# A PEER decoder layer on one core: 42 instead of 32 dense tokens leave the dense down products, and VectorE forms five of the last lower halves

## The reference, cut to what matters

```python
SEQ, D_MODEL, PEER_HEADS, PEER_TOPK, PEER_N_EXPERTS = 512, 1024, 8, 16, 16384

# short convolution and HGRN2 heads -> output projection -> cross-attention into 256 memory tokens, then:
h = rmsnorm(x, ffn_norm_w)
x = x + peer_ffn(h, w_query, sub_keys, expert_down, expert_up)
return rmsnorm(x, final_norm_w)

def peer_ffn(...):
    # per token and head: top 16 of each half of the keys, then the top 16 of the 256 pairs, softmax gates
    u = jnp.take(expert_down, idx, axis=0)                 # 128 rows of 1024 for each token
    a = jax.nn.gelu(jnp.einsum('nd,nhkd->nhk', xb, u))
    w = gb * a
    v = jnp.take(expert_up, idx, axis=0)
    return jnp.einsum('nhk,nhkd->nd', w, v)
```

## Time and profile before

| | us |
|---|---|
| median of 3 runs (1622.50 to 1630.98) | 1624.84 |
| the profiled execution | 1624.01 |
| its span, first to last instruction | 1622.3 |
| TensorE busy | 1600.3 |
| VectorE busy | 1133.7 |
| GpSimd busy | 829.1 |
| ScalarE busy | 673.2 |

### The profile page before, as it was taken

One profiled execution on the slowest core, in us unless ns is written; L12 is line 12 of the kernel. 1 busy time (PEld: TensorE's weight loads), 2 busy tenths in 40 slices (PEclk: granted clock), 3 DMA queues, 4 the chain that ended last, 5 costly groups with the idle time before them and its releaser, 6 DMA issues.

```text
span 1622.3 us, 26556 instructions
## 1 busy us (share of the span) xinstructions
PE 1600.3 (99%) x9227; PEld 1422.6 (88%) x9227; DVE 1133.7 (70%) x2214; ACT 673.2 (41%) x998; POOL 829.1 (51%) x523
## 2 busy tenths in 40 slices
PE   8999999999999999999999999999999999999998
PEld 6888888788889999999999999998888888888886
DVE  4155451351509999996999898329888888888887
ACT  5342453451534343534545544444333333333333
POOL 4463276423244998987787777866422222222220
PEclk9999999999999999999999999999999999999999
DMA  4322242313434999997999999949999999999992
GB/s 184 93 100 71 75 151 94 104 53 117 146 102 131 347 340 332 329 335 233 339 405 394 387 403 401 362 158 391 400 348 350 331 349 339 349 334 348 339 331 77
DMA packets 154425, 424.69 MB, mean 262 GB/s; under 512 B 15728, under 2 KB 65904, under 8 KB 154224
## 3 DMA queue, kind: packets, MB, share of 16 engines
q1 hardware_dynamic: 89088, 229.41, 40.5%
q0 software_dynamic: 41472, 151.01, 25.5%
q10 hardware_dynamic: 23792, 43.33, 6.9%
HBM read 379.88 MB, written 43.25 MB: 261 GB/s over the span
## 4 chain that ended last, share of the span: by engine, by line
PE 69%; issue 16%; POOL 9%; DVE 2%; DMA 2%; ACT 1%; POOLq 0%; SPq 0%; ACTq 0%; DVEq 0%
PE psum L1471 22%; PE psum L1473 22%; PE psum L1472 22%; POOL w_low L461 8%; PE psum L1766 4%; DMA gate_dram<-arena 1%; DMA kept<-down_in 1%; POOL arena L493 1%; DMA arena<-down_rows,arena 0%; DVE arena L1258 0%; ACT w_high L581 0%; DVE arena L1202 0%; DVE arena L1193 0%; DVE arena L1194 0%; DMA kept<-front_w 0%
## 5 line engine op out<-in xcount | busy, mean ns | idle before, releaser
L461 POOL TENSOR_TENSOR w_low<-kept,w_high 128x1024 fp32r<-128x1024 f32 x212 | 519.5, 2454 | 320.3 <-ACT w_high L581 317.6
L1471 PE MATMUL psum<-hT_high,w_high 128*128 128x352 f32 (+2 forms) x1408 | 484.4, 344 | 7.2 <-POOL w_low L461 5.5
L1473 PE MATMUL psum<-hT_high,w_low 128*128 128x352 f32 (+2 forms) x1408 | 476.6, 339 | 0.0
L1472 PE MATMUL psum<-hT_low,w_high 128*128 128x352 f32 (+2 forms) x1408 | 476.4, 338 | 0.0
L581 ACT ACTIVATE w_high<-kept 128x1024 fp32r<-128x1024 f32 x212 | 224.0, 1058 | 202.6 <-DMA kept<-down_in 102.0
L1471 PE MATMUL psum<-up_high,wgt_high 128*128 128x512 f32 x768 | 298.8, 389 | 0.0
L1473 PE MATMUL psum<-up_high,wgt_low 128*128 128x512 f32 x768 | 298.8, 389 | 0.0
L1472 PE MATMUL psum<-up_low,wgt_high 128*128 128x512 f32 x768 | 298.8, 389 | 0.0
L1471 PEld LDWEIGHTS psum<-hT_high,w_high 128*128 128x128 f32 x1408 | 264.8, 188 | 24.2 <-POOL w_low L461 8.2
L1473 PEld LDWEIGHTS psum<-hT_high,w_low 128*128 128x128 f32 x1408 | 264.7, 188 | 12.7
L1472 PEld LDWEIGHTS psum<-hT_low,w_high 128*128 128x128 f32 x1408 | 264.8, 188 | 12.3 <-issue 0.5
(11 more groups left out here) (252 smaller groups left out, 1956.4 us busy)
## 6 DMA issues: line engine op xcount, KB each, us to landing
kept<-down_in SPq DMA_DIRECT2D x128, 512.0 KB
arena<-up_in SPq DMA_DIRECT2D x128, 512.0 KB, 4.7
kept<-front_w SPq DMA_DIRECT2D x92, 512.0 KB
gate_dram<-arena ACTq DMA_DIRECT2D x40, 512.0 KB
hid_dram<-arena ACTq DMA_DIRECT2D x112, 176.0 KB
arena<-hid_dram SPq DMA_DIRECT2D x112, 176.0 KB
under_w<-gate_dram SPq DMA_DIRECT2D x24, 640.0 KB
arena<-gate_dram SPq DMA_DIRECT2D x8, 640.0 KB
```

Source lines behind the costliest of these rows:

```text
L461: nc.gpsimd.tensor_tensor(w_low[:, s, :], ring[:, s, :], w_hi[:, s, :].bitcast(F32), ALU.subtract).then_inc(low_ready, 1)
L1471: nc.tensor.matmul(out, lhs[0], rhs[0], start=first, stop=False)
L1472: nc.tensor.matmul(out, lhs[0], rhs[1], start=False, stop=False)
L1473: return nc.tensor.matmul(out, lhs[1], rhs[0], start=False, stop=last)
```

## The change

EDGE goes from 32 to 42. The dense block is then 128 x 342, three groups of 42 tokens fill 126 partitions, and their 128 slots go into 43 gathers (43 + 43 + 42), which read 126 rows, the last one 84. ROWS goes from 160 to 171. The dots move between the stretches: 70 instead of 66 by the end of the early stretch (four more, DOTS_LULL, stand after the last choice, but their gathers are spread over the same blocks 2 to 53), 76 instead of 80 in the gate steps, 25 instead of 14 in the last blocks. VectorE makes the lower halves of blocks 109, 111, 113, 115 and 117 (`dve_low`) and TensorE waits for them by a semaphore of their own. GELU of the edge dots moves to step 16, the wait for its results to step 23. Each of the three small groups of DMAs has three transfers of 42 partitions for four of 32. TensorE's last 20 blocks are written out instead of a loop. Nothing else differs.

```diff
-EDGE = 32
+EDGE = 42
-EDGE_SLOTS = SLOTS // PARTS
+EDGE_SLOTS = -(-SLOTS // PARTS)
-E0, E_BASE = P - EDGE, P - 32
+E0, E_BASE = P - EDGE, P - 64
-GEL_AT, SPLIT_AT, LAST_TURN = 12, 20, 28
+GEL_AT, SPLIT_AT, LAST_TURN = 16, 23, 28
-DOTS_A = DT * (sum(DOTS_SCORES) + sum(DOTS_CAND) + DOTS_HOT)
-DOTS_STEP = (0, 0) + (2,) * 10 + (1, 2, 2) * 12
-DOTS_END = (1,) * 14
+DOTS_LULL = 4
+DOTS_A = DT * (sum(DOTS_SCORES) + sum(DOTS_CAND) + DOTS_HOT) + DOTS_LULL
+DOTS_STEP = (0, 0, 1) + (2, 2, 1) * 15
+DOTS_END = (2, 2) * 6 + (1,)
...
+        def dve_low(i):
+            return DURING <= i < DURING + 10 and i % 2 == 1
...
-                nc.gpsimd.indirect_dma_start(ring[slot], None, down_rows, bass.IndirectOffsetOnAxis(
-                    (edge_idx if edge else idx3)[:, j:j + 1].bitcast(U32), 0))\
+                rows = edge_rows(j) if edge else P
+                nc.gpsimd.indirect_dma_start(ring[slot][0:rows], None, down_rows, bass.IndirectOffsetOnAxis(
+                    (edge_idx if edge else idx3)[0:rows, j:j + 1].bitcast(U32), 0))\
...
-                low(FRONT + i, i % 4)
+                if not dve_low(i):
+                    low(FRONT + i, i % 4)
...
+            kd = dots(kd, DOTS_LULL)
             assert kd == DOTS_A
...
-            kd = dots(kd, ROWS - kd)
+            for i in range(DURING, DURING + len(DOTS_END)):
+                if dve_low(i):
+                    dve.wait_ge(high_ready, FRONT + i + 1)
+                    nc.vector.tensor_tensor(w_low[:, i % 4, :], ring[:, i % 4, :], w_hi[:, i % 4, :].bitcast(F32),
+                                            ALU.subtract).then_inc(end_low_ready, 1)
+                kd = dots(kd, DOTS_END[i - DURING])
...
-            with pe.Fori(DURING // 4, NK // 4) as r:
-                for s in range(4):
-                    first_product(r * 4 + s, s)
+            for i in range(DURING, NK):
+                if dve_low(i):
+                    pe.wait_ge(end_low_ready, sum(dve_low(j) for j in range(i + 1)))
+                first_product(i, i % 4, FRONT + sum(not dve_low(j) for j in range(i + 1)))
```

More of the change, by code:

```diff
@@ L214, in build @@
         hk_last, split_last = at(136.25, 2 * P, 2, P), at(26, 3 * P, 3, P)
-        edge_idx, edge_dot, edge_gel = (at(137.25 + 0.125 * j, EDGE_SLOTS) for j in range(3))
+        edge_idx, edge_dot, edge_gel = (at(137.25 + 0.25 * j, EDGE_SLOTS) for j in range(3))
         idx_last, edge_back = at(17, SLOTS), at(18, SLOTS)
@@ L253, in build @@
         high_ready = sem("high_ready")
-        low_ready = sem("low_ready")
+        low_ready, end_low_ready = sem("low_ready"), sem("end_low_ready")
         idx_ready = sem("idx_ready")
@@ L325, in __call__, with part_slots, part_count, edge_rows @@
                 self.end()
+        def dve_low(i):
+            return DURING <= i < DURING + 10 and i % 2 == 1
+        def part_slots(q):
+            return slice(q * EDGE_SLOTS, min((q + 1) * EDGE_SLOTS, SLOTS))
+        def part_count(q):
+            return min(EDGE_SLOTS, SLOTS - q * EDGE_SLOTS)
+        def edge_rows(j):
+            return EDGE * sum(j < part_count(q) for q in range(PARTS))
         block = ctx.enter_context(nc.Block())
@@ L1181, in dots @@
                         step(nc.vector.tensor_copy(h_chunks, own_h))
-                    nc.vector.tensor_tensor_reduce(ring[slot], ring[slot], h_row, 1.0, 0.0, ALU.mult, ALU.add,
-                                                   (edge_dot if edge else dot3)[:, j:j + 1]).then_inc(dot_done, 1)
+                    rows = edge_rows(j) if edge else P
+                    nc.vector.tensor_tensor_reduce(ring[slot][0:rows], ring[slot][0:rows], h_row[0:rows], 1.0, 0.0, ALU.mult, ALU.add,
+                                                   (edge_dot if edge else dot3)[0:rows, j:j + 1]).then_inc(dot_done, 1)
                 return first + count
@@ L1473, in three, with columns @@
                 return nc.tensor.matmul(out, lhs[1], rhs[0], start=False, stop=last)
-            def columns(b, s, rhs, n, bank):
-                pe.wait_ge(low_ready, b + 1)
+            def columns(b, s, rhs, n, bank, lows=None):
+                pe.wait_ge(low_ready, b + 1 if lows is None else lows)
                 for k in range(KC):
```

39 lines of the change are left out of this document (23 added, 16 removed).

## The result

The changed kernel takes 1663.8 us (median of 6 runs, 1648.0 to 1669.3) where the kernel before takes 1627.5 (6 runs): a ratio of 1.021, 95% interval 1.0187 to 1.0234. The forecast was 1627, its range ended at 1636. The prediction was wrong in size: it had the kernel 2.6 us slower and it is 36.3 us slower.

The account below looks back on a forecast made before the run. TensorE was taken as the bound, with GpSimd just behind in the early and last blocks. The terms +3.7 - 4.7 + 3.4 + 0.2 = +2.6 gave 1627 us on the median; forecast 1622 to 1631 (0.56), range 1614 to 1636.

Parts of the forecast that it names:

- Ten columns fewer: TensorE's first products: 0.42 ns a column, 0.10 us a block, 12.8 us less over 128 blocks.
- Early stretch, +3.7: Blocks 0 to 59: GpSimd's added gathers and dot waits outweigh the shorter products, 3.7 us longer.
- the dot waits of gathers 32 and 54: Early stretch: GpSimd waits for dots ahead of these moved gathers, about 2.9 us near 611 and 3.3 near 684.
- The prediction is wrong if the early stretch ends before 759: Test set for the early stretch: an end before 759 us would refute the prediction.
- Gate steps, -4.7: Blocks 60 to 107: TensorE's period falls from 5.29 to 5.19 us, less 0.1 for stores of gates: 4.7 us shorter.
- -4.8 to -3.5: Bounds in us given for the change of the gate steps, blocks 60 to 107.
- Last blocks, +3.4: Last 20 blocks: shorter products give -2.0, the ring of four row buffers and VectorE's halves +5.4: 3.4 us longer.
- The cycle of the ring: Last blocks: four gathers, or two blocks, take landing plus 1.7 us, 9.4 us for GpSimd's 7.5 of work.
- the landing: Last blocks: time from a gather's issue until its row is taken up, put at 7.7 us from bytes moved.
- far bound (+8.9): Last blocks: with a landing of 8.9 us they come 8.9 us longer.
- Two SBUF inputs: VectorE's new lower halves beside GpSimd's: each up to 2.2 us more, but 0.4 us taken for all.
- "Slower": Rival: the ring of four row buffers decides in the last blocks, +8.9 us in sum, 1634 us; chance 0.16.

Follow-up runs that it names:

- e2: The kernel before the change, with its 32 edge gathers reading 126 rows instead of 128: ratio 1.0080.
- e9: The kernel before the change, with TensorE's first products 342 columns wide and 352 columns still moved: ratio 0.9972.
- e10: The kernel before the change, with hidden rows stored and loaded 342 columns wide (1368 bytes), products still 352 wide: ratio 1.0027.
- e3: The changed kernel, with hidden rows at a pitch of 1408 bytes in memory instead of 1368, 342 columns still moved: ratio 1.0158.
- e11: e1 with hidden rows stored and loaded 352 columns wide (1408 bytes): ratio 1.0077.
- e13: e12 with as many dots in the early stretch and gate steps as before the change (66 and 80, then 25): ratio 0.9998.
- e1: The changed kernel, with each of its 43 edge gathers reading 128 rows: ratio 1.0139.
- after: The changed kernel itself, compared with the kernel before: 1663.8 us, ratio 1.021.
- e6: e1 with GpSimd making all lower halves of the last blocks, none on VectorE: ratio 1.0142.
- e12: e11 with the 25 last dots placed as 2, 1, 2 over 15 blocks: ratio 1.0068.
- e8: e1 with the 25 last dots placed as 2, 1, 2 over 15 blocks instead of 2 a block over 12: ratio 1.0114.
- e14: e13 with a ring of eight row buffers instead of four from block 112 on: ratio 0.9998.
- e5: e1 with all gathers but the first of each ring, and their dots, on 64 partitions instead of 128: 1641.8 us, one run.

## Why the prediction was wrong, step by step

**What bounds the kernel.** The busy shares and the chain pointed at TensorE and GpSimd, and that is where the prediction looked. It read the DMA share only for the gate steps and the last blocks. In the early stretch it was 0.94 to 0.99 up to 720 us, and the argument should have started there: with transfer engines that full, e2 shows what a transfer that gets worse costs: 0.8%.

**Ten columns fewer: mis-sized.** 0.10 us a block predicted, 0.05 measured. 128 blocks give 6 us, not 12.8. e9 alone gives 4.6 us.

**Early stretch, +3.7: the failing step is what the sum left out.** No term of it was a transfer. The edge gathers were taken as 43 like any others, though the text says that they read 126 rows, and the narrower hidden tile was not costed at all. The first is 11.3 of the 19.2 us (257.2 against 245.9 without it), and e10 puts the second at 5.3 us in this stretch of the old kernel, one profile each. By the medians of the whole kernel they are 0.7% and 0.5 to 0.6%. The way in which they cost is not in the prediction either: ScalarE waits 40.3 us for stores of the hidden tile where it waited 0.9, and 77.9 us for loads where it waited 73.0 (523 to 760 us). The terms that were there, the dot waits of gathers 32 and 54, were right in place and near in size, as e3 and e11 show, but in the changed kernel late high halves covered the first and part of the second (2.07 of 3.3 us). "The prediction is wrong if the early stretch ends before 759" named the wrong side: it ended at 780.5.

**Gate steps, -4.7: right where nothing disturbs.** The period fell to 5.23 us (5.19 predicted, the rest is the column price), 48 of them are 251.0, and e9, e11 and e13 reach 251.3 to 251.6. In the changed kernel 8.5 us are lost on top of the 251.0. 2.7 of them fall in blocks 60 to 75, where the last 126-row gathers are issued (until block 69); e2 loses 6.0 there. Most of the rest are the stores of gates, for which I gave back 0.1 us. They come as single stalls: here in e1, behind block 101, ScalarE waiting for a store, TensorE for ScalarE.

```profile
991.35 0.60 ACT L919 ACTIVATE arena<-psum 128x512 f32<-128x512 f32 x1 [6.10 <-DMA gate_dram<-arena]
...
992.00 0.86 PE L1796 MATMUL psum<-arena 128*128 128x128 bf16 x12 [3.24 <-ACT arena L919]
```

Such a stall costs 2 to 5 us, behind block 93 or 101 in after, e1, e6 and e12 and behind block 77 in e8; in e9, e11 and e13 it doesn't occur. "-4.8 to -3.5" was too narrow for that.

**Last blocks, +3.4: right sign, the cause at best in part.** The cycle of the ring was forecast at 9.4 us for four gathers. In e1 12 gathers, from 1031.32 to 1064.90, take 33.6 us, 11.2 for four, so the cycle was under-sized too. But e14 took the ring away from block 112 on and won 1.0 us. The bytes that I had used to size the landing held up the loads too, and those stand on TensorE's path directly. That +9.0 came out next to the far bound (+8.9) is luck. In the changed kernel itself, where the ring, the rows and the loads act together, their shares were not parted.

**Two SBUF inputs, 0.4 us: hardly met.** The five halves on VectorE took 1.22 us each in e1, and taking them away changed nothing beyond the intervals. But none of the five ran beside a lower half of GpSimd there, and in after only 0.1 us of one did. Where one did it was held up, as the prediction's row had it. In e5 a half started 1.15 us into one of GpSimd's and took 2.32 us:

```profile
1038.10 2.37 POOL L474 TENSOR_TENSOR w_low<-kept,w_high 128x1024 fp32r<-128x1024 f32 x1
```

```profile
1039.25 2.32 DVE L1373 TENSOR_TENSOR w_low<-kept,w_high 128x1024 fp32r<-128x1024 f32 x1
```

In e13 one took 1.65. The rule of the Trainium skill ("GPSIMD Engine Reference", section "8. Key points") that speaks against this part is borne out by these rows; it cost little because the two engines' halves mostly miss each other.

**The rivals.** "Slower" was there with 0.16 and 1634, nearly all of it in the last blocks. There was no rival for the transfers, which the diff showed in one line, `ring[slot][0:rows]`.

## What to carry to other kernels

Where the DMA share is as high as here (0.94 to 0.99), cost every transfer whose shape changes, also where it gets smaller: two rows fewer of 128 cost 0.8%, ten columns fewer 0.3%, and with both padded back and the gathers in their old places nothing of the loss was left. Look for the second bound behind the one that is removed: the four moved gathers cost 0.25% at most until the hidden rows were mended, and then 0.7%. This also tells how to read a run that mends one thing and gains little: e3 had removed one bound and met the next, which its total hid and its waits showed. And interpolate a price only between rows that lie near: 0.42 ns a column holds from 512 to 352 and from 352 to 256, and between 352 and 342 it was half that.

No version that computes everything beat the kernel before: e13 is at 0.9998. In e13's profile the last blocks, where eleven more gathers have to land, take 4.6 us more than before, as much as the shorter products give in e9.

## What the runs showed of the hardware that I had not expected

- A gather of 126 rows costs more than one of 128, and not only itself: packets of the block loads beside it took 0.195 us instead of 0.169.
- Gathers into 64 partitions instead of 128, with half the bytes, did not shorten the early stretch: from 560 to 600 us the loads' packets went from 0.181 to 0.223 us, and the share stayed at 0.99.
- Stored and loaded rows of 1368 bytes cost 0.27%, rows of 1344 and 1408 nothing. A pitch of 1408 around 1368 bytes took ScalarE's wait for the stores from 40.3 to 5.6 us and 0.5% off the time (1.0158 for 1.0210, intervals touching).
- A lower half on VectorE takes 1.22 us alone and up to 2.32 where it starts beside one of GpSimd's.
- A product of 338 columns ran at 155.4 ns in one block and at 160.0 in another, at a full clock in both.
- After an idle stretch TensorE's next products can run at the lower clock. In e1 the stall behind block 101 was followed by a granted clock of 0.72 over 6.1 us, a mixture of its two levels (1.2 and 2.4 GHz), and block 102 took 5.4 us for 3.86:

```profile
992.00:998.10 6.10, 6.10 (x37) 5.97 (x38) 5.37 (x9) 3.87 (x6) 4.18 (x3) 0.72 0.95 349
```

  A stall of 3.2 us so costs 4.8. It doesn't follow each time: after 2.4 us ahead of block 53 in the changed kernel the block took its 3.88.
